# Halved first weights, input transposes ahead of all products, an earlier second weight group, and gate chunks in four loads

## What is computed

```python
for l in range(2):
    h = x @ w_in[l]                                  # 1024 -> 2336
    out_a, out_b, out_c = three attention groups on columns of h
    mix = jnp.concatenate([out_a, out_b, out_c], axis=-1) @ w_o[l]
    x = layer_norm(ALPHA * x + mix, ln1_g[l], ln1_b[l])
    # product-key mixer: 8 heads, each picks 16 of 16384 experts per token
    q = x @ w_q
    sc = scores of q against the sub keys; top 16 x top 16 -> 16 experts, gates = softmax
    act = gelu(<u[expert], x>)
    ffn = sum(gates * act * v[expert])
    x = layer_norm(ALPHA * x + ffn, ln2_g[l], ln2_b[l])
```

## Time and profile before

| | us |
|---|---|
| median of 3 runs | 3362.67 |
| lowest and highest run | 3360.81, 3369.53 |
| the profiled execution, its time | 3367.06 |
| its span, first to last instruction | 3365.2 |
| TensorE busy in it | 3226.9 (96%) |
| VectorE, ScalarE, GpSimd busy | 2505.9, 1298.0, 1959.8 |

### The profile page before, as it was taken

One profiled execution on the slowest core, in us unless ns is written; L12 is line 12 of the kernel. 1 busy time (PEld: TensorE's weight loads), 2 busy tenths in 40 slices (PEclk: granted clock), 3 DMA queues, 4 the chain that ended last, 5 costly groups with the idle time before them and its releaser, 6 DMA issues. The chain is left out here.

```text
span 3365.2 us, 64277 instructions
## 1 busy us (share of the span) xinstructions
PE 3226.9 (96%) x18452; PEld 2941.0 (87%) x18454; DVE 2505.9 (74%) x5425; ACT 1298.0 (39%) x2046; POOL 1959.8 (58%) x1554
## 2 busy tenths in 40 slices
PE   7999899999999999999989998999999999999997
PEld 7888789999999888778788887899999998887886
DVE  1366467888888788888924565678888888888888
ACT  2355234444444333333323542344444443333332
POOL 3445337888654466666544453388886544666665
PEclk9999999999999999999989999999999999999999
DMA  4101128999787799999730011399997877999996
GB/s 153 40 1 63 39 81 275 321 320 321 246 298 251 266 321 325 336 328 322 269 113 25 1 76 38 91 300 321 319 319 246 293 249 271 326 335 333 323 323 216
DMA packets 248633, 765.15 MB, mean 227 GB/s; under 512 B 27617, under 2 KB 94945, under 8 KB 240609
## 3 DMA queue, kind: packets, MB, share of 16 engines
q1 hardware_dynamic: 169632, 459.94, 41.3%
q0 software_dynamic: 73728, 268.47, 21.2%
q10 hardware_dynamic: 5184, 35.65, 2.9%
HBM read 677.98 MB, written 85.98 MB: 227 GB/s over the span
## 5 line engine op out<-in xcount | busy, mean ns | idle before, releaser
L670 POOL TENSOR_TENSOR st_lo<-st_raw,st_hi 128x1024 fp32r<-128x1024 f32 x290 | 697.4, 2405 | 468.4 <-ACT st_hi L923 464.2
L1823 PE MATMUL ps<-t_hi,st_hi 128*128 128x384 f32 (+1 forms) x2304 | 801.3, 348 | 5.8 <-DVE t_lo L1096 5.8
L923 ACT CAST st_hi<-st_raw 128x1024 fp32r<-128x1024 f32 x544 | 569.7, 1047 | 613.4 <-PE ps L1906 613.3
L1824 PE MATMUL ps<-t_lo,st_hi 128*128 128x384 f32 (+1 forms) x2304 | 792.7, 344 | 0.0
L778 POOL TENSOR_TENSOR wt_lo<-w_f,wt_hi 128x384 fp32r<-128x384 f32 x256 | 391.2, 1528 | 334.9 <-ACT wt_hi L1038 334.8
L1827 PE MATMUL ps<-t_hi,st_lo 128*128 128x384 f32 (+1 forms) x2304 | 466.0, 344 | 0.0
L1823 PEld LDWEIGHTS ps<-t_hi,st_hi 128*128 128x128 f32 x2304 | 433.2, 188 | 17.1 <-issue 6.2
L1824 PEld LDWEIGHTS ps<-t_lo,st_hi 128*128 128x128 f32 x2304 | 433.2, 188 | 10.5
L1827 PEld LDWEIGHTS ps<-t_hi,st_lo 128*128 128x128 f32 x2304 | 411.6, 188 | 11.4
L1906 PE MATMUL ps<-st_hi,wt_hi 128*128 128x512 f32 x1536 | 391.7, 390 | 11.8 <-ACT wt_hi L1038 11.8
L1906 PE MATMUL ps<-st_lo,wt_hi 128*128 128x512 f32 x1536 | 391.6, 390 | 6.4 <-DVE st_lo L1498 6.4
(11 more groups left out here) (211 smaller groups left out, 5047.5 us busy)
## 6 DMA issues: line engine op xcount, KB each, us to landing
st_raw<-in_peer_u SPq DMA_DIRECT2D x256, 512.0 KB, 4.9
st_raw<-in_peer_v SPq DMA_DIRECT2D x256, 512.0 KB, 4.6
gelu_d<-h_out SPq DMA_DIRECT2D x256, 192.0 KB
h_in<-gelu_d SPq DMA_DIRECT2D x256, 192.0 KB, 5.4
gates_d<-g_stage ACTq DMA_DIRECT2D x32, 1024.0 KB, 5.9
g_ch<-gates_d SPq DMA_DIRECT2D x14, 2048.0 KB, 11.6
w_raw<-in_w_in SPq DMA_DIRECT2D x16, 1168.0 KB, 5.2
st_raw<-in_peer_w_q SPq DMA_DIRECT2D x32, 512.0 KB, 3.6
```

Source lines behind the costliest of these rows:

```text
L670: nc.gpsimd.tensor_tensor(st_lo[:, s].rearrange("p c f -> p (c f)"), st_raw[:, r], st_hi[:, s].rearrange("p c f -> p (c f)").bitcast(F32), ...
L923: nc.scalar.copy(st_hi[:, r % 2].rearrange("p c f -> p (c f)"), st_raw[:, r]).then_inc(st_h, 1)
L1823: nc.tensor.matmul(dst, st_hi[:, s, c], t_hi[:, c, rows], start=c == 0, stop=False)
L1824: nc.tensor.matmul(dst, st_hi[:, s, c], t_lo[:, c, rows], start=False, stop=False)
```

## The change

In the first group's weights (of both layers) ScalarE's cast and GpSimd's subtraction are each cut into two halves of four depth chunks, with new semaphores `first_hi` and `first_lo` for the first half. TensorE waits for `first_lo` before the first product, and for `wc_lo` before depth chunk 4 of the first token block. In layer 0 all four token blocks are transposed before the first product; in layer 1 the transposes stay between the products. In layer 1 ScalarE casts group 1's weights between token blocks 1 and 2, and the loop of ScalarE is rolled so that the cast of group 1 stands ahead of it. The weight loads of a layer no longer wait for `st_used`. Each gate chunk is loaded in four loads, one for each of the four token windows: for chunk 0 in a row, for the others one ahead of each `quad`.

```diff
-            sp.wait_ge(st_used, ST_PER * l + PRIME)
             sp.wait_ge(v_acc, SLOTS * l + 1)
...
-            sp.dma_start(g_ch[:, :, 0:GCH], gates_d[:, :, LEAD:LEAD + GCH]).then_inc(s_gch[0], 16)
+            for w in range(2 * WIN_D):
+                sp.dma_start(g_ch[:, w, 0:GCH], gates_d[:, w, LEAD:LEAD + GCH]).then_inc(s_gch[0], 16)
...
-            sp.dma_start(g_ch[:, :, GCH:2 * GCH], gates_d[:, :, LEAD + GCH:LEAD + 2 * GCH]).then_inc(s_gch[1], 16)
...
+            def chunk(c, slot, size=GCH):
+
                 sp.wait_ge(wt_f, EB * l + GCH * (c - 1) + LEAD + PRIME)
...
+                sp.sem_inc(waited, 1)
+                with sp.Fori(0, per_ch) as w:
+                    sp.dma_start(g_ch[:, ds(w, 1), slot * GCH:slot * GCH + size],
+                                 gates_d[:, ds(w, 1), ds(GCH * c + LEAD, size)]).then_inc(s_gch[slot], 16)
+                    quad((c - 1) * per_ch + w + 1)
+
+            with sp.Fori(0, EB // GCH // 2 - 1) as c:
+                chunk(2 * c + 1, 1)
+                chunk(2 * c + 2, 0)
+            chunk(EB // GCH - 1, 1, GCH - LEAD)
...
+            def rest_first(l):
+
+                half = DC * IN_N // 2
+                for k, (ready, done) in enumerate(((first_hi, first_lo), (wc_hi, wc_lo))):
+                    cols = slice(k * half, (k + 1) * half)
+                    pool.wait_ge(ready, l + 1 if k == 0 else W_PER * l + 1)
+                    nc.gpsimd.tensor_tensor(w_lo[:, 0, cols], w_raw[:, 0, cols], w_hi[:, 0, cols].bitcast(F32),
+                                            ALU.subtract).then_inc(done, 1)
...
+            def round_first(l):
+
+                half = DC * IN_N // 2
+                act.wait_ge(s_wraw[0], 16 * (W_PER // 2 * l + 1))
+                act.wait_ge(pj_ps, TB * (W_PER * l + 1))
+                for k, done in enumerate((first_hi, wc_hi)):
+                    cols = slice(k * half, (k + 1) * half)
+                    nc.scalar.copy(w_hi[:, 0, cols], w_raw[:, 0, cols]).then_inc(done, 1)
...
-                round_group(0, 0, DC * IN_N)
+                round_first(0)
                 for tb in range(TB):
                     round_tokens(0, tb)
+                round_group(1, 1, DC * IN_N)
+            keep_h(0, 0)
             with act.Fori(0, IN_G // 2 - 1) as i:
-                round_group(2 * i + 1, 1, DC * IN_N)
-                keep_h(2 * i, 0)
                 round_group(2 * i + 2, 0, DC * IN_N)
                 keep_h(2 * i + 1, 1)
-            round_group(IN_G - 1, 1, DC * IN_N)
+                round_group(2 * i + 3, 1, DC * IN_N)
+                keep_h(2 * i + 2, 0)
...
-            keep_h(IN_G - 2, 0)
             keep_h(IN_G - 1, 1)
...
-                dve.wait_ge(s_gch[slot], 16 * (EB // GCH // 2 * l + c + 1))
+                dve.wait_ge(s_gch[slot], 16 * 2 * WIN_D * (EB // GCH // 2 * l + c + 1))
...
-                pe.wait_ge(wc_lo, W_PER * l + n + 1 + PRIME)
+                if between is None:
+                    pe.wait_ge(wc_lo, W_PER * l + n + 1 + PRIME)
...
-                        if between is not None and c == DC // 2 and tb + 1 < TB:
+                        if between is not None and c == 0 and tb == 0:
+                            pe.wait_ge(first_lo, l + 1)
+                        if between is not None and c == DC // 2 and tb == 0:
+                            pe.wait_ge(wc_lo, W_PER * l + n + 1 + PRIME)
+                        if between is not None and c == DC // 2 and tb + 1 < TB and l > 0:
                             between(tb + 1)
...
-                        turn_input(0)
+                        for tb in range(TB if l == 0 else 1):
+                            turn_input(tb)
                         group(n, s, IN_N, 0, turn_input)
```

More of the change, by code:

```diff
@@ L325, in build @@
     wc_hi, wc_lo = sem("wc_hi"), sem("wc_lo")
+    first_hi, first_lo = sem("first_hi"), sem("first_lo")
     pj_ps, pj_act, pj_dve, pj_res = sem("pj_ps"), sem("pj_act"), sem("pj_dve"), sem("pj_res")
@@ L486, in _ @@
             per_ch = GCH // RAW
-            with sp.Fori(1, per_ch + 1) as i:
-                quad(i)
-            with sp.Fori(1, EB // GCH // 2 - 1) as c:
-                for slot in range(2):
-                    sp.wait_ge(wt_f, EB * l + GCH * (2 * c + slot - 1) + LEAD + PRIME)
-                    sp.dma_start(g_ch[:, :, slot * GCH:(slot + 1) * GCH],
-                                 gates_d[:, :, ds(GCH * (2 * c + slot) + LEAD, GCH)]).then_inc(s_gch[slot], 16)
-                    with sp.Fori(1, per_ch + 1) as k:
-                        quad(c * (2 * per_ch) + k + (slot - 1) * per_ch)
-            for slot in range(2):
-                c = EB // GCH - 2 + slot
-                size = GCH if slot == 0 else GCH - LEAD
-                sp.wait_ge(wt_f, EB * l + GCH * (c - 1) + LEAD + PRIME)
-                sp.dma_start(g_ch[:, :, slot * GCH:slot * GCH + size],
-                             gates_d[:, :, GCH * c + LEAD:GCH * c + LEAD + size]).then_inc(s_gch[slot], 16)
-                with sp.Fori((c - 1) * per_ch + 1, min(c * per_ch + 1, EB // RAW - 1)) as i:
-                    quad(i)
+            assert per_ch == 2 * WIN_D
+            def chunk(c, slot, size=GCH):
+                sp.wait_ge(wt_f, EB * l + GCH * (c - 1) + LEAD + PRIME)
+                sp.sem_inc(waited, 1)
[7 more added lines that the diff above has]
+            chunk(EB // GCH - 1, 1, GCH - LEAD)
             with sp.Fori((EB // GCH - 1) * per_ch + 1, EB // RAW - 1) as i:
@@ L525, in _, with rest_group @@
         for l in range(L):
-            def rest_group(n, s, size, l=l):
+            def rest_first(l):
[5 more added lines that the diff above has]
+                                            ALU.subtract).then_inc(done, 1)
+            def rest_group(n, s, size):
                 pool.wait_ge(wc_hi, W_PER * l + n + 1)
@@ L532, in _ @@
             if l == 0:
-                rest_group(0, 0, DC * IN_N)
+                rest_first(0)
             rest_group(1, 1, DC * IN_N)
@@ L800, in _ @@
             if l + 1 < L:
-                rest_group(0, 0, DC * IN_N, l + 1)
+                rest_first(l + 1)
             norm_tail(1)
@@ L1058, in _ @@
             if l + 1 < L:
-                round_group(0, 0, DC * IN_N, l + 1)
+                round_first(l + 1)
             act.wait_ge(ln_scaled, 2 * l + 2)
@@ L1067, in _ @@
             if l + 1 < L:
-                for tb in range(1, TB):
+                round_tokens(3 * l + 3, 1)
+                act.wait_ge(s_wraw[1], 16 * (W_PER // 2 * (l + 1) + 1))
+                act.wait_ge(pj_ps, TB * (W_PER * (l + 1) + 2))
+                nc.scalar.copy(w_hi[:, 1, 0:DC * IN_N], w_raw[:, 1, 0:DC * IN_N]).then_inc(wc_hi, 1)
+                for tb in range(2, TB):
                     round_tokens(3 * l + 3, tb)
```

2 lines of the change are left out of this document (1 added, 1 removed).

## The result

| | runs | us, median | lowest to highest |
|---|---|---|---|
| before | 4 | 3362.8 | 3360.8 to 3369.5 |
| after | 4 | 3325.4 | 3324.4 to 3326.8 |

The ratio is 0.9886, its 95% interval 0.9869 to 0.9903. The spans of the two profiled executions are 3365.2 and 3322.9 us. The kernel before ran again beside the experiments: over all 33 of its runs the median is 3365.2 (3360.0 to 3369.7), so the runs that stood beside the prediction showed it some 2.5 us faster than it is on the whole. The changed kernel, run again beside the last three experiments, took 3326.3 us against 3366.4, ratio 0.9881. The gain is 37 to 40 us.

A forecast was written before the change was run, and what follows sets the result against it. TensorE, busy in 96% of the span, was taken to bound the kernel. Gains of 24.5 (value stages), 8.2 (start) and 4.6 us (passage), 37.3 together, took the median from 3362.67 to 3325.4 us; range 3317 to 3338.

The forecast's parts named there:

- Value stage: Last stage of each layer: gate chunks in four pieces end TensorE's fourteen stops, 25.3 us lost; gain 24.5 us.
- the spare of h_in: Value stage: an h_in load takes 5.5 us in quiet stretches and so has 1.1 us to spare.
- the cover of VectorE: Value stage: blocks computed ahead let VectorE be 4.3 us late before TensorE stops.
- the 0.8 us that I took off for the first piece: Value stage: 0.8 us deducted because chunk 1's first piece falls into the stage's start, where first loads are caught up.
- (a): Value stage: pieces keep half of the 25.3 us loss, VectorE cannot catch up between pieces; 3337.3 us, chance 0.10.
- (b): Value stage: each piece costs what a chunk did, 101.4 us in place of 25.3; 3426 us, chance 0.03.
- Start: Start of layer 0: transposes first, group 1 starts at 33.5 instead of 41.73 without a wait; gain 8.2 us.
- rival (c): Start of layer 0: clock stays low through all of group 0, no gain there; 3333.6 us, chance 0.04.
- Passage: Layer 0 to layer 1: sequence runs 2.0 us earlier and group 1's 2.66 us wait goes; gain 4.6 us.
- The 1.07 us that I ascribed to the half cast: Passage to layer 1: POOL waits for only half of ScalarE's cast, 1.07 us less.
- Rival (d): Passage to layer 1: gives nothing, because x_tok[1] waits for something else no earlier; 3330 us, chance 0.04.
- The premise that time won early is kept to the end: Whole kernel: outside three places TensorE's rows follow at a fixed step and nothing waits for a clock time.

## Why the prediction was right

**Value stage, 24.5 forecast, 25.0 measured.** The mechanism held: the queue delay of h_in by the bytes ahead of it, the spare of h_in, the cover of VectorE. With 2 MB, 1 MB and 0.5 MB ahead of h_in TensorE's stops cost 25, 0 and 0 us. One size was off. A whole chunk delayed h_in by 6.3 us (11.7 less 5.4; I had 7.0), a quarter by 0.8 and not by the 1.75 that bytes in proportion gave, so it mostly stays within the spare of 1.1 us. That is why VectorE hardly waited, where I had expected many short waits. Of the 0.8 us that I took off for the first piece, 0.3 were lost in all. Rivals (a) and (b) fall.

**Start, 8.2 forecast, 11.1 measured at lat_n.** The forecast time of group 1 was 33.5, it came at 33.45, so the gain up to there is 8.3. The first product was 0.7 later than said (19.66: the last block of x landed at 18), the clock rose sooner (7 slow products instead of 20); the two errors cancel, and rival (c) falls. The step that was missing lies behind: I costed the wait of 2.65 us at its own length and took group 1 behind it as unchanged. In the profiled execution of before its first 24 products ran at the lower clock, 24 x (0.24 - 0.136) = 2.5 us, and the whole group took 15.7 us against 12.9 after. The rows were there to be read (the earlier trace rows ends with a product of 0.58 us where 0.40 stands elsewhere).

**Passage, 4.6 forecast, 5.0 measured up to group 1, 6.6 at lat_n.** The second transposes moved by 1.9 us (2.0 said), the wait of 2.66 went, and the clock, which rose during the second transposes (1.68 us in place of 1.97), gave most of the other 0.4. Behind group 1 the same term is missing, 1.6 us. GpSimd starts 2.1 us sooner, counted from the value stage, where I said 2.0. What I didn't see is the collision with VectorE's ln_shift that the earlier start causes. The 1.07 us that I ascribed to the half cast are there (GpSimd starts 6.6 us behind the value stage with whole weights, 5.7 with halves), but the halves did more: they ended that collision after 2.65 us of GpSimd's time instead of 5.1. With whole weights the earlier loads cost more than they bring, by the traces: the second transposes stand at 18.8 us without the wait of SyncE and at 17.5 with it. The medians, 3329.2 and 3327.3, point the same way without showing it. Rival (d) falls.

**The sum.** The forecast of 3325.4 met the median to 0.1 us, and that is luck. Up to group 1 and over the value stages the two traces give 8.3 + 5.0 + 25.0 = 38.3 us, against 37.3 forecast. The missing term, clock lost behind the two waits, adds 2.8 + 1.6 = 4.4 us in them. By the medians the gain is 39.8 us against the 33 runs of before, which leaves some 1.5 us for that term, as fits a fall of the clock that comes only in some executions. The forecast, 2.5 us too small by this, started from a median of three runs that was 2.5 us low, and the two errors cancelled.

The premise that time won early is kept to the end held within 1.2 us: the stages between, which the change does not touch, lasted 1003.7 and 1006.1 us in place of 1004.6 and 1004.9.

## What to carry to other kernels

Where a large load and small urgent ones share a queue, cut the large one only until its piece delays the small one by less than the consumer's cover, and put work of the small kind between the pieces: cutting alone won nothing. Price a wait of TensorE with what its clock may lose behind it, and treat that part as chance. When GpSimd work is moved, look for what VectorE issues in that moment with two operands in SBUF, since a one-column instruction that comes 0.3 us too late stands until the GpSimd instruction ends.

## What the hardware showed that I had not expected

**The same code at another clock.** Between lat_n and the value stage all kernels run the same instructions, yet fourteen profiled executions give 1003.7 to 1009.8 us for it in layer 0. Two windows of that stage (columns as in the earlier trace rows), of after and of the kernel with the first weights whole:

```profile
310.00:330.00 20.00, 15.15 (x128) 14.77 (x128) 7.69 (x10) 8.02 (x8) 9.18 (x2) 1.00 0.82 315
...
380.00:400.00 20.00, 17.03 (x93) 14.42 (x92) 6.80 (x12) 8.16 (x11) 4.78 (x2) 1.00 0.18 54
```
```profile
310.00:330.00 20.00, 16.81 (x128) 16.43 (x128) 7.78 (x10) 7.68 (x7) 9.19 (x2) 0.91 0.83 315
...
380.00:400.00 20.00, 17.29 (x74) 14.23 (x72) 6.09 (x10) 6.00 (x7) 4.77 (x2) 0.80 0.13 36
```

In the second, TensorE issued 74 matmuls in 20 us where the first issued 93, at 0.80 of its clock (by then the second is also some us behind in its work). A few stretches at the lower level, in places where TensorE is only partly busy, come in one execution and not in the next. In this stage they add up to 13.6 us in the shortest of the fourteen, which is after, and to 30.8 in the longest. But 20.5 us of them stand in a stage of 1004.6 us and in one of 1007.4, so they are part of the 6 us and not shown to be all of it. An experiment of one or two us must be read in its own stage, not in its total.

The trace of the kernel before has such stretches too. So the clock is not below full speed only at the start and at the passage, as "Time and profile before" says, and TensorE's rows do not follow each other at a fixed step everywhere outside the three places, as the prediction has it:

```profile
380.00:400.00 20.00, 8.44 (x45) 7.70 (x46) 17.34 (x16) 5.89 (x6) 8.74 (x3) 0.74 0.02 3
```

**Whose instruction starts first.** 0.3 us decide between 0.16 and 4.79 us for VectorE's ln_shift, as shown above. The gate multiplication w_f, whose two inputs lie in SBUF as well, obeys the same rule. GpSimd and VectorE in a quiet block of the kernel before:

```profile
1196.43 1.64 POOL L778 TENSOR_TENSOR wt_lo<-w_f,wt_hi 128x384 fp32r<-128x384 f32 x1 [1.32 <-ACT wt_hi L1038]
```
```profile
1197.12 1.24 DVE L1488 TENSOR_TENSOR w_f<-g_ch,h_in 128x256 f32<-128x256 f32 x1
```

Over layer 0's value stages of before and after, 505 us of each, 215 of 246 rows of w_f start while GpSimd's wt_lo is running. All but one, which starts in wt_lo's last 0.2 us, take 0.81 to 1.24 us and end 0.3 us behind it. The 31 others take 0.41 to 0.46 us, as behind the stop in the earlier trace rows. Before, 29 of 121 were of this kind, because VectorE was late behind each stop; after, 2 of 125. So the mean rose from 1045 to 1203 ns because the stops are gone, and VectorE's cover hides it in this kernel.
